# Norms of a decoder step: sums of squares in four column tiles, root and reciprocal on 136 columns, spread by four small products

## What is computed

```python
def rms_norm(x, g):
    x32 = x.astype(F32)
    y = x32 * lax.rsqrt(jnp.mean(x32 * x32, axis=-1, keepdims=True) + RMS_EPS)
    return (y * g.astype(F32)).astype(x.dtype)

def layer_forward(x, c, pos, lw, conv_buf, h0, attn_fn):
    ...
    f = swiglu(rms_norm(x, g[0]) * (1 + sc1) + sh1, w_gu[0], w_dn[0])
    x = x + 0.5 * gt1 * rms_norm(f, g[1])
    h = rms_norm(x, g[2]) * (1 + sc2) + sh2
    ...
    y = jnp.concatenate([y_lru, y_att.astype(h.dtype)], axis=-1) @ w_o
    x = x + gt2 * rms_norm(y, g[3])
    f = swiglu(rms_norm(x, g[4]) * (1 + sc3) + sh3, w_gu[1], w_dn[1])
    x = x + 0.5 * gt3 * rms_norm(f, g[5])
```

## Time and profile before

| | |
|---|---|
| runs, median (lowest to highest) | 3206.49 us (3205.24 to 3208.41) |
| profiled execution, its own time | 3210.13 us |
| its span, first to last instruction | 3208.6 us |
| mean granted TensorE clock | 0.835 |
| PE busy | 2761.5 us (86%), 20638 products |
| DVE busy | 1464.7 us (46%) |
| ACT busy | 783.2 us (24%) |
| POOL busy | 159.5 us (5%) |
| L556, sums of squares, 384 records | 102.8 us of PE |
| L859, root, 12 | 8.6 us of ACT |
| L1121 and L1149, reciprocals, 6 and 6 | 21.3 and 21.3 us of DVE |

### The profile page before, as it was taken

How to read it: one execution, slowest core, us unless ns; L and a number is a source line. 1 busy time by engine, 2 the same in 40 slices (tenths; PEclk the granted TensorE clock), 3 DMA queues, 4 the chain that set the end, 5 groups by cost and what they waited for, 6 DMA issues and landing times.

```text
span 3208.6 us, 56345 instructions
## 1 busy us (share of the span) xinstructions
PE 2761.5 (86%) x20638; PEld 2556.8 (80%) x20638; DVE 1464.7 (46%) x2006; ACT 783.2 (24%) x1076; POOL 159.5 (5%) x299
## 2 busy tenths in 40 slices
PE   5999797987769679999969998979796786799997
PEld 3999796976546569999959997969674566699997
DVE  3333124365799553332243331154648984533312
ACT  2333023220012233322223321222200222333221
POOL 0000001001330000000000000010113200000000
PEclk9999798985555789999969997989655558899998
DMA  6223622212354113222342226323123531123221
GB/s 189 85 85 89 182 86 85 75 43 61 107 148 121 41 40 89 88 83 73 96 122 87 85 85 185 91 70 82 49 59 114 156 92 53 40 85 91 73 81 64
DMA packets 524666, 291.19 MB, mean 91 GB/s; under 512 B 20545, under 2 KB 518882, under 8 KB 524162
## 3 DMA queue, kind: packets, MB, share of 16 engines
q1 hardware_dynamic: 513154, 266.45, 28.5%
q0 software_dynamic: 11392, 23.23, 2.4%
HBM read 285.85 MB, written 3.77 MB: 90 GB/s over the span
## 4 chain that ended last, share of the span: by engine, by line
PE 77%; issue 8%; DVE 7%; DMA 3%; SPq 2%; ACT 2%; DVEq 0%; POOLq 0%; POOL 0%; ACTq 0%
PE ps L583 60%; PE ps L704 4%; PE ps L556 3%; PE ps L702 3%; DMA sb_wslot<-w_ada 3%; PE ps L594 2%; PE ps L603 1%; PE ps L566 1%; ACT sb_h L865 1%; PE ps L724 1%; DVE sb_h L1150 1%; PE ps L747 1%; PE ps L768 1%; SPq L436 1%; SPq L434 1%
## 5 line engine op out<-in xcount | busy, mean ns | idle before, releaser
L583 PE MATMUL ps<-sb_h_lo,sb_w_hi 128*128 128x272 f32 x3360 | 696.8, 289 | 0.0
L875 ACT ACTIVATE sb_w_hi<-sb_wslot 128x1024 fp32r<-128x1024 f32 (+2 forms) x322 | 333.1, 1037 | 1445.3 <-PE ps L583 1313.7
L1111 DVE TENSOR_TENSOR sb_w_lo_ffn<-sb_wslot,sb_w_hi 128x1024 fp32r<-128x1024 f32 (+1 forms) x272 | 324.1, 1194 | 778.5 <-ACT sb_w_hi L875 778.0
L583 PE MATMUL ps<-sb_h_hi,sb_w_hi 128*128 128x272 f32 x2816 | 585.6, 289 | 48.6 <-DVE sb_h_lo L1136 48.6
L583 PE MATMUL ps<-sb_h_hi,sb_w_lo_ffn 128*128 128x272 f32 x2816 | 585.3, 289 | 0.0
L583 PEld LDWEIGHTS ps<-sb_h_lo,sb_w_hi 128*128 128x128 f32 x3360 | 531.5, 190 | 0.0
L583 PEld LDWEIGHTS ps<-sb_h_hi,sb_w_hi 128*128 128x128 f32 x2816 | 445.7, 189 | 50.3 <-issue 50.2
L583 PEld LDWEIGHTS ps<-sb_h_hi,sb_w_lo_ffn 128*128 128x128 f32 x2816 | 442.0, 190 | 0.0
L583 PE MATMUL ps<-sb_act_hi,sb_w_hi 128*128 128x272 f32 x1408 | 294.5, 291 | 11.1 <-DVE sb_w_lo_ffn L1111 11.1
L583 PE MATMUL ps<-sb_act_lo,sb_w_hi 128*128 128x272 f32 x1408 | 293.7, 290 | 0.0
L583 PE MATMUL ps<-sb_act_hi,sb_w_lo_ffn 128*128 128x272 f32 x1408 | 293.6, 290 | 0.0
(11 more groups left out here) (218 smaller groups left out, 3235.0 us busy)
## 6 DMA issues: line engine op xcount, KB each, us to landing
sb_wslot<-ffn_w_gu SPq DMA_DIRECT2D x176, 512.0 KB, 3.7
sb_wslot<-w_ada SPq DMA_DIRECT2D x144, 512.0 KB, 5.2
sb_wslot<-ffn_w_down SPq DMA_DIRECT2D x64, 512.0 KB, 3.6
sb_wslot<-w_in SPq DMA_DIRECT2D x32, 512.0 KB, 3.7
sb_wslot<-ffn_w_down SPq DMA_DIRECT2D x32, 384.0 KB, 3.1
sb_down<-key_pages POOLq DMA_DIRECT2D x128, 96.0 KB, 2.2
sb_down<-key_pages SPq DMA_DIRECT2D x128, 96.0 KB, 2.0
sb_wslot<-w_out SPq DMA_DIRECT2D x16, 512.0 KB, 4.0
```

The lines of the kernel that those rows point to most:

```text
L583: last = mm(ps[:, 2 * pair + b, 0:TH], weights, moving[:, kc, b * TH:(b + 1) * TH], start=first, stop=final)
L875: act_fn(w_hi[s][:, 0:rows, 0:cols], wslot[i][:, 0:rows, 0:cols], ACT.Copy).then_inc(w_hi_done.sem, 1)
L1111: v.tensor_tensor(w_lo[s][:, 0:rows, 0:cols], wslot[i][:, 0:rows, 0:cols], w_hi[s][:, 0:rows, 0:cols].bitcast(F32), ALU.subtract).then_inc ...
```

## The change

Three things change in every norm. The sums are taken in four column tiles: a weight block of ones with only 32 columns, and for each chunk four products of 136 columns (`TQ`), each for a quarter of the tokens into its own 32 partitions of bank 6. So partitions 0 to 31 hold the sums of the first quarter of the tokens, 32 to 63 those of the second, and so on. Root and reciprocal then run on 128 x 136. At last PE spreads the reciprocals over all partitions: for each quarter one product of a single row of ones with a single row of reciprocals, each in its own row tile of the array, into banks 4 to 7. DVE multiplies straight out of these banks. Two semaphores are new: `inverse_ready` from DVE to PE and `spread_ready` from PE to DVE.

```diff
+TQ = T // 4
...
+        root_4 = rinv[:, 0:TQ]
...
+        inverse_ready = sig("inverse_ready", 6)
+        spread_ready = sig("spread_ready", 6)
...
-            def sums_of_squares(squares, l, k):
+            def sums_of_squares(squares, l, k, n):
...
                 for c in range(DC):
                     pe.wait_ge(squares.sem, squares.at(l, k + c + 1))
-                    for b in range(2):
-                        last = mm(ps[:, 6 + b, 0:TH], ones, sq[:, c, b * TH:(b + 1) * TH],
+                    for g in range(4):
+                        last = mm(ps[g * CW:(g + 1) * CW, 6, 0:TQ], ones[:, 0:CW], sq[:, c, g * TQ:(g + 1) * TQ],
                                   start=(c == 0), stop=(c == DC - 1))
                 last.then_inc(ss_ready.sem, 1)
+                hold(pe, passed[1], inverse_ready.sem, inverse_ready.at(l, n + 1))
+                for g in range(4):
+                    last = mm(ps[:, 4 + g, 0:TQ], ones[g * CW:g * CW + 1, :],
+                              root_4[g * CW:g * CW + 1, :], start=True, stop=True)
+                last.then_inc(spread_ready.sem, 1)
...
-                act_fn(tok2(rinv[:, :]), halves(3), ACT.Sqrt, bias=eps[:, 0:1], scale=1.0 / D).then_inc(root_ready.sem, 1)
+                act_fn(root_4, ps[:, 6, 0:TQ], ACT.Sqrt, bias=eps[:, 0:1], scale=1.0 / D).then_inc(root_ready.sem, 1)
...
-                    st.link(v.reciprocal(rinv[:, :], rinv[:, :]))
+                    v.reciprocal(root_4, root_4).then_inc(inverse_ready.sem, 1)
+                    dve.wait_ge(spread_ready.sem, spread_ready.at(l, r + 1))
                     for c in range(DC):
-                        v.tensor_tensor(h[:, c, :], x[:, c, :], rinv[:, :], ALU.mult).then_inc(xn_ready.sem, 1)
+                        v.tensor_tensor(tok4(h[:, c, :]), tok4(x[:, c, :]), ps[:, 4:8, 0:TQ], ALU.mult)\
+                            .then_inc(xn_ready.sem, 1)
...
-                    st.link(v.reciprocal(rinv[:, :], rinv[:, :]))
-                    st.link(v.tensor_tensor(h[:, :, :], h[:, :, :], rinv[:, :].unsqueeze(1).to_broadcast([P, DC, T]),
+                    v.reciprocal(root_4, root_4).then_inc(inverse_ready.sem, 1)
+                    dve.wait_ge(spread_ready.sem, spread_ready.at(l, r + 1))
+                    h2 = h[:, :, :].rearrange("p c (b t) -> p c b t", b=4)
+                    st.link(v.tensor_tensor(h2, h2, ps[:, 4:8, 0:TQ].unsqueeze(1).to_broadcast([P, DC, 4, TQ]),
                                             ALU.mult))
```

More of the change, by code:

```diff
@@ L125 @@
 KREC = PAGE + PAGE // 2
-DVE_STEPS = 361
+DVE_STEPS = 355
 class Signal:
@@ L423, in halves, with tok4 @@
             return ps[:, 2 * pair:2 * pair + 2, 0:TH]
+        def tok4(v):
+            return v.rearrange("p (b t) -> p b t", b=4)
         def tok2(v):
@@ L641, in _ @@
                 ada(l, ADA0, 0, 2)
-                sums_of_squares(sq_ready, l, 0)
+                sums_of_squares(sq_ready, l, 0, 0)
                 ffn(l, 0, GU1, DN1, lambda: ada(l, ADA1, 2, 5))
-                sums_of_squares(dn_read, l, 0)
-                sums_of_squares(sq_ready, l, 8)
+                sums_of_squares(dn_read, l, 0, 1)
+                sums_of_squares(sq_ready, l, 8, 2)
                 def swapped(c):
@@ L838, in _ @@
                         piece(OUT, u, n, n % 2, w_lo_mid, y_hi, y_lo)
-                sums_of_squares(wo_read, l, 0)
-                sums_of_squares(sq_ready, l, 16)
+                sums_of_squares(wo_read, l, 0, 3)
+                sums_of_squares(sq_ready, l, 16, 4)
                 ffn(l, 1, GU2, DN2, lambda: None)
-                sums_of_squares(dn_read, l, 8)
+                sums_of_squares(dn_read, l, 8, 5)
         @block.scalar
```

## The result

The changed kernel takes **3133.95 us** (median of four runs, 3131.81 to 3134.56) against 3207.43 for the kernel before beside it: ratio 0.9771, 95% interval 0.9754 to 0.9788, so 73.5 us less. The forecast was 3135. The profiled execution took 3131.81, its span is 3130.2; the spans of the two profiled executions lie 78.4 us apart (3208.6 and 3130.2).

A forecast was written before the change was run, and what follows sets the result against it. Dense product work bounds most of the span (PE 77% of the chain), with twelve norms whole on the path; savings of 41.7, 15.0 and 15.0, together 71.7 us, take 3206.5 to 3135 us, range 3120 to 3160.

The forecast's parts named there:

- The sums: Each norm's sums of squares on PE: 7.35 us at full clock become 2.07, or 3.87 at half clock.
- Tiles at once: Sums on PE: four column tiles run at once, as adaLN's 32 products do in 1.95 us at 2.4 GHz.
- The rival without concurrent column tiles: Sums' column tiles run in turn; only root, reciprocal and spread count, 23 us saved, 3184 us; chance 0.05.
- Root and reciprocal: ACT's root and DVE's reciprocal in each norm, on 136 columns: 715 ns to 0.37 us, 3553 ns to 0.99 us.
- The spread: New step between reciprocal and multiply, PE spreading reciprocals: 0.9 us in residual norms, 1.3 in the six others.
- low ends: Reciprocal to multiply if the four row tiles run at once: 0.54 us at full clock, 0.76 at half.
- the 71.7: Total us saved over twelve norms: 41.7 in six residual norms, 15.0 in four pre-norms, 15.0 in two first norms.
- The multiply from PSUM: DVE's multiply in each norm, reading four PSUM banks: 54 multiplies x 8 ns, taken as nothing.
- the slower rival: Each norm's multiply from four banks costs 1.37 ns more an element, eating the gain; 3248 at three times today's price; chance 0.03.
- Late next: Next late step: table load in residual norms, DVE's two subtractions in pre-norms behind a residual, sums in first norms.
- The rival of a later return to 2.4 GHz: Six products behind pre-norms stay longer at half clock, losing 3 us each, 18 us: 3153 us; chance 0.08.
- 1595.7, still earlier: End of layer 0: PE's spread is over at 1595.7, so layer 1's adaLN products, today at 1598.20, are not delayed.

The follow-up runs named there:

- tiles_in_turn: The changed kernel with the same 32 narrow products of a norm's sums ordered one column tile after the other: 3177.11 us, ratio 0.9899.
- one_row_tile: The changed kernel with all four spread products taken from row tile 0, so every quarter is scaled with the first quarter's reciprocals: 3150.38 us, ratio 0.9817.
- table_ahead: The changed kernel with a one-element root on ACT behind its last split of a down or output product, loading the table early: 3131.18 us, ratio 0.9764.
- root_first: The changed kernel with root and reciprocal ahead of the pre-norms' weight splits and subtractions, one subtraction moved into the split of h: 3130.82 us, ratio 0.9767.
- hold_alone: The kernel before with one wait of PE added behind a layer's last sums, for that norm's root: 3210.91 us, ratio 1.0012.

## Why the prediction was right, and where it was not

**The sums.** "2.07 us" at full clock was measured as 2.07 at norm 1, and the first norms' sums, taken as 3.87, as 3.69 and 3.85. Tiles at once, from the adaLN row, was the step that carried most of the forecast, and tiles_in_turn shows it: when the same products go tile by tile, 42.9 us of the norms' gain are lost. The rival without concurrent column tiles put that at 3184, the run gave 3177.

**Root and reciprocal.** 0.37 and 0.99 us were forecast by a line through two sizes. The instructions of the two lines in the changed kernel, grouped by shape (busy us, mean ns | idle before):

```profile
L871 ACT ACTIVATE sb_rinv<-ps,sb_eps 128x136 f32<-128x136 f32 x12 | 4.4, 367 | 7.1 <-PE ps L563 7.1
...
L1163 DVE RECIPROCAL sb_rinv<-sb_rinv 128x136 f32<-128x136 f32 x6 | 6.0, 1003 | 70.4 <-ACT sb_rinv L871 70.4
```

**The spread.** Taken as 0.9 and 1.3 us between reciprocal and multiply, measured as 0.72 (the idle in front of L1166, 4.3 us in six) and, at half clock, 1.04. The first norm of layer 0 had the full clock at its spread, and 0.72 too. These are the mis-sized terms, toward the low ends of 0.54 and 0.76, and at 6 x 0.18 + 5 x 0.26 + 0.58 = 3.0 us they account for nearly all of the 3.1 that the norms gained beyond the 71.7. The low ends counted the eight records as an eighth of 64, 0.26 and 0.48 us; they took 0.51 and 0.83, and the handing over 0.21 both times where 0.28 was taken. The Trainium skill, TensorEngine Tiling (Array Packing), Key Properties, has different tiles multiply in parallel; one_row_tile agrees, 0.51 us against 1.18.

**The multiply from PSUM.** Forecast at no cost; the view of one line's instructions (count, ns least/median/most) has for the two, first before, then in the changed kernel:

```profile
L1123 DVE TENSOR_TENSOR sb_h<-sb_x,sb_rinv x48: 717/719/726, 65.6 to 2770.7; 128x544 f32<-128x544 f32 x48
...
L1150 DVE TENSOR_TENSOR sb_h<-sb_h,sb_rinv x6: 4691/4693/4693, 533.4 to 3190.6; 128x4352 f32<-128x4352 f32 x6
```

```profile
L1136 DVE TENSOR_TENSOR sb_h<-sb_x,ps x48: 710/712/722, 56.7 to 2699.8; 128x544 f32<-128x544 f32 x48
...
L1166 DVE TENSOR_TENSOR sb_h<-sb_h,ps x6: 4686/4688/4689, 515.7 to 3111.3; 128x4352 f32<-128x4352 f32 x6
```

The medians fell from 719 to 712 and from 4693 to 4688 ns. So the slower rival is out. The Trainium skill, Perfetto Trace Analysis, Optimizing Scalar/DVE Operations, has a dearer access to PSUM, by an estimate from its two figures 65 ns for each of these; this form of multiply doesn't show it, since they became shorter by 5 to 7.

**Late next.** What the forecast named as the next step to be late was right in each kind of norm. The table load in the residual norms, DVE's subtractions in the pre-norms, the sums in the first norms: all three show in the chain or the table above, and table_ahead and root_first move the first two.

**The clock.** The rival of a later return to 2.4 GHz, 3 us in each product, did not happen: the heads of the six products are 16.92 us in the mean before and 16.96 after, 0.2 us in all, and the granted clock was back at 1.00 after 4.0 us in the mean before and 4.1 after (one execution of each).

**The step that failed: the layer boundary.** "1595.7, still earlier" was wrong. I counted from the last square to the end of the spread and let the adaLN products follow at once. The timeline of PE at the end of layer 0 of the changed kernel:

```profile
1560.85 0.51 PE L568 MATMUL ps<-sb_rinv,sb_cst 1*128 1x136 f32 x8 [2.05 <-DVE sb_rinv L1163]
1565.15 3.64 PE L606 MATMUL ps<-sb_wslot,sb_cT 128*32 128x128 f32 x64 [3.79 <-issue]
```

Between spread and adaLN lie 3.79 us in which PE waits for nothing but its own stream. The jump back to the layer's start stands there, and the trace has its time, on PE's sequencer (PEldq). The view of the loop's line (ns least/median/most, first and last start) at the end of layer 0, first before, then the changed kernel, then hold_alone:

```profile
L639 PEldq COMPARE_BRANCH  x1: 3362/3362/3362, 1594.1 to 1594.1; - x1
```

```profile
L651 PEldq COMPARE_BRANCH  x1: 3717/3717/3717, 1561.0 to 1561.0; - x1
```

```profile
L639 PEldq COMPARE_BRANCH  x1: 3505/3505/3505, 1600.3 to 1600.3; - x1
```

The jump is not new, and hardly longer. Before, PE's stream got to it without having to wait for DVE; it took its 3.36 us from 1594.10 to 1597.46, while the last sums ran (until 1598.28), and adaLN began with the last sum, with no idle. In the changed kernel it starts behind the spread's wait, and PE has no products left to run beside it. Now adaLN starts 7.17 us behind the last square (1557.98), where it was 6.08 (1592.12 to 1598.20) and I had forecast 3.6. The loads that adaLN frees come later with it, and run into DVE's own jump. Rows of the chain at DVE's jump ("issue") and the first copy behind it, with the multiply ahead of them where it stands in the chain; first before, then the changed kernel, then hold_alone:

```profile
1602.65 4.70 DVE sb_h L1150
...
1613.91 2.77 issue
...
1617.19 0.70 DVE sb_modT L1199
```

```profile
1572.67 4.89 issue
...
1578.07 0.70 DVE sb_modT L1215
```

```profile
1603.68 4.70 DVE sb_h L1151
...
1614.94 4.92 issue
...
1620.38 0.70 DVE sb_modT L1200
```

From the multiply (1561.42 in the changed kernel) to that copy it takes 14.54 us before, 16.65 in the changed kernel and 16.70 in hold_alone; DVE's jump alone makes 2.12 and 2.15 of it. It takes 4.10 to 5.53 us in all eleven runs that have PE wait ahead of its own jump, hold_alone among them. hold_alone also has the hole in PE's stream:

```profile
1604.29 3.64 PE L594 MATMUL ps<-sb_wslot,sb_cT 128*32 128x128 f32 x64 [4.98 <-issue]
```

The first 0.76 of its 4.98 us are the wait for the root (1599.31 to 1600.07), the other 4.22 the jump and what the sequencer does around it. So the hold by itself makes most of the loss, 2.16 of the 2.58 us, without anything else of the change. The windows over DVE's jump, before and after, show what stands beside it (length, busy us of PE, PEld, DVE, ACT and POOL, granted clock, DMA share, GB/s):

```profile
1613.91:1616.68 2.77, 0.00 (x0) 0.00 (x0) 0.00 (x0) 0.34 (x1) 0.00 (x0) 0.50 0.09 27
```

```profile
1572.67:1577.56 4.89, 2.50 (x40) 1.19 (x32) 0.00 (x0) 0.34 (x1) 0.00 (x0) 0.50 1.13 336
```

And the DMA view of the same stretch in the changed kernel has code among the transfers (queue: packets, MB, share of 16 engines):

```profile
q1 hardware_dynamic: 3215, 1.62, 111.7%
q8 instruction: 1, 0.02, 1.2%
q14 instruction: 1, 0.01, 0.4%
```

Two packets of code also pass in PE's hole of 3.79 us, and one in DVE's 2.77 before. The Trainium skill, Runtime: NRT & Kernel Launch, Instruction fetch mechanics, has a taken branch wait for its target page to be fetched by DMA, when that isn't at hand. The rows agree: each jump has its packet, and DVE's, with the weights' loads beside it, takes 2.1 us longer, in two kernels. That the loads are what lengthens it was not tested apart. The step was costed at nothing, and a program with more layers would pay it at each boundary between two.

**Luck in the total.** 3135 came within about 1 us of the measured 3133.95, closer than its terms deserve: the norms gave 3.1 us more than the 71.7 forecast, and the layer boundary and the program's end took back 3.5 that the forecast put at nothing.

## What to carry to other kernels

Small products in several tiles of the array leave the path only if consecutive products go to different tiles: the same 32 products took 2.07 us in turns over four tiles and 6.24 one tile after the other. When a long step shrinks, read from the timeline what comes last next in each kind of place, a table load, another queue, a subtraction, and sum the gain to that and no further; work moved behind it must then fit in front of its own reader, chunk by chunk. A wait that is put in front of a loop's jump exposes the jump (here 3.36 us beside the sums became 3.72 with PE idle), and delays all that the first instructions behind it set free.

## What was not expected of the hardware

- Column tiles in turn are three times as slow as four at once, not four times (6.24 against 2.07 us for 64 records), since four records of each tile start beside the last four of the tile ahead.
- Products with one weight row in four row tiles run at once: 0.51 us at full clock and 0.83 at half for eight records, against 1.18 and 2.15 from one row tile.
- A loop's jump took PE's sequencer 3.36 us beside running products, and 3.72 and 3.50 behind a wait, where PE stood still; DVE's took 2.77 us with the DMA engines at a share of 0.09 and 4.89 and 4.92 beside weight loads.
- A one-element root loads the table ahead, and the copy and square behind it don't bring another load; it is then wholly beside the product (root 0.89 us behind the last square, not 1.31).
